# A third weight buffer from the first query on, four row buffers instead of five until the values, two engines' unit loops written out

## What is computed

```
q   = xn @ w_query                       # 8 heads, 2 x 128 each
s   = q . sub_keys                       # top 16 of 128, twice, then top 16 of 256
idx = e1 * 128 + e2                      # 8 x 16 experts of 16384 for each token
act = gelu(xn . expert_u[idx])
out = sum(gate * act * expert_v[idx])
```

## Time and profile before

| | |
|---|---|
| median of 3 runs | 4069.86 us (4068.22 to 4072.91) |
| profiled execution, its own time | 4066.02 us |
| span in its profile | 4063.9 us |
| PE busy in matmuls | 3865.1 us, 95% of the span |
| POOL / DVE / ACT busy | 2352.7 / 2448.9 / 1338.7 us |
| moved by DMA | 958.97 MB, mean 236 GB/s |
| mean granted clock of PE | 0.983 |

### The profile page before, as it was taken

One profiled execution on the slowest core, in us unless ns is written; L12 is line 12 of the kernel. 1 busy time (PEld: TensorE's weight loads), 2 busy tenths in 40 slices (PEclk: granted clock), 3 DMA queues, 4 the chain that ended last, 5 costly groups with the idle time before them and its releaser, 6 DMA issues.

```text
span 4063.9 us, 67270 instructions
## 1 busy us (share of the span) xinstructions
PE 3865.1 (95%) x27521; PEld 3420.8 (84%) x27521; DVE 2448.9 (60%) x3532; ACT 1338.7 (33%) x1380; POOL 2352.7 (58%) x994
## 2 busy tenths in 40 slices
PE   7999999999999999989999989999988999999997
PEld 5777777777778777869999989899988999999997
DVE  4343344433473555146878789986446777776776
ACT  4332233322332222123333334443233333333333
POOL 5332233322333344436666676667778999998995
PEclk8999999999999999989999999999999999999999
DMA  3222222222222344235676789999989999998994
GB/s 116 103 77 82 89 87 84 82 89 82 83 98 99 110 147 161 97 122 217 257 277 259 276 334 421 421 359 369 371 327 406 405 398 407 399 406 326 415 406 175
DMA packets 216723, 958.97 MB, mean 236 GB/s; under 512 B 18328, under 2 KB 92312, under 8 KB 114352
## 3 DMA queue, kind: packets, MB, share of 16 engines
q1 hardware_dynamic: 126832, 478.30, 32.1%
q0 software_dynamic: 55296, 402.68, 24.0%
q10 hardware_dynamic: 34368, 74.69, 4.7%
HBM read 891.01 MB, written 64.52 MB: 235 GB/s over the span
## 4 chain that ended last, share of the span: by engine, by line
PE 64%; POOL 11%; DMA 10%; DVE 7%; issue 3%; ACT 2%; SPq 1%; ACTq 0%; POOLq 0%; DVEq 0%
PE ps L417 17%; PE ps L419 16%; PE ps L418 16%; POOL wl L408 6%; DMA rowb<-v_rows,idx 4%; DMA raw<-stream 3%; POOL wl L412 3%; PE ps L1706 2%; PE ps L2029 2%; DVE ps L1451 2%; PE ps L2031 1%; PE ps L2030 1%; DVE H L1448 1%; DMA stage<-v_rows,idx 1%; POOL rowb L686 1%
## 5 line engine op out<-in xcount | busy, mean ns | idle before, releaser
L412 POOL TENSOR_TENSOR wl<-raw,wh 128x2048 fp32r<-128x2048 f32 x268 | 1242.7, 4637 | 1441.8 <-ACT wh L393 1440.6
L417 PE MATMUL ps<-xh,wh 128*128 128x320 f32 (+1 forms) x3904 | 1420.8, 364 | 87.3 <-POOL wl L412 62.3
L419 PE MATMUL ps<-xh,wl 128*128 128x320 f32 (+1 forms) x3904 | 1375.0, 352 | 0.0
L418 PE MATMUL ps<-xl,wh 128*128 128x320 f32 (+1 forms) x3904 | 1374.6, 352 | 0.0
L417 PEld LDWEIGHTS ps<-xh,wh 128*128 128x128 f32 x3904 | 742.1, 190 | 192.4 <-issue 66.8
L393 ACT ACTIVATE wh<-raw 128x2048 fp32r<-128x2048 f32 x270 | 517.1, 1915 | 939.6 <-PE ps L419 737.9
L419 PEld LDWEIGHTS ps<-xh,wl 128*128 128x128 f32 x3904 | 741.5, 190 | 83.0
L418 PEld LDWEIGHTS ps<-xl,wh 128*128 128x128 f32 x3904 | 742.9, 190 | 81.2 <-issue 7.7
L2029 PE MATMUL ps<-gah,wh 128*128 128x320 f32 x2048 | 645.7, 315 | 55.3 <-POOL wl L408 23.7
L2031 PE MATMUL ps<-gah,wl 128*128 128x320 f32 x2048 | 634.7, 310 | 0.0
L2030 PE MATMUL ps<-gal,wh 128*128 128x320 f32 x2048 | 634.6, 310 | 0.0
(11 more groups left out here) (334 smaller groups left out, 3986.6 us busy)
## 6 DMA issues: line engine op xcount, KB each, us to landing
raw<-stream SPq DMA_DIRECT2D x396, 1024.0 KB
gelu_scratch<-preb ACTq DMA_DIRECT2D x128, 160.0 KB
gates_scratch<-stage ACTq DMA_DIRECT2D x10, 2048.0 KB
gt<-gates_scratch SPq DMA_DIRECT2D x32, 640.0 KB
act<-gelu_scratch SPq DMA_DIRECT2D x32, 640.0 KB
mergegate_scratch<-sgb ACTq DMA_DIRECT2D x32, 256.0 KB, 2.0
sgm<-mergegate_scratch SPq DMA_DIRECT2D x32, 256.0 KB, 2.7
h_in<-x_t SPq DMA_DIRECT2D x4, 1024.0 KB, 7.8
```

Of the source, the lines that this page charges most:

```text
L412: pool.tensor_tensor(wl[s][:, :], raw[s][:, :], wh[s][:, :].bitcast(F32), ALU.subtract).then_inc(w_lo, 1)
L417: pe.matmul(dst, w_h, h[:, kx, lo:], start=start, stop=False)
L418: pe.matmul(dst, w_h, l[:, kx, lo:], start=False, stop=False)
L419: return pe.matmul(dst, w_l, h[:, kx, lo:], start=False, stop=stop)
```

## The change

The third buffer takes the memory of `rowb1` and serves from unit 124 on; `rowb1` moves to memory that `stage[0]` and a part of `stage[1]` hold until the gates are stored, and serves from j = 69 on. Up to j = 68 four row buffers are left, the quarters of H, so that fetch(n) waits for use(n - 4). Since the buffer of a unit is now its number modulo three, SP's loads and ACT's head and gate loops are written out. PE's loops and the order of `USED` are as before.

```
-    homes = range(ROWS_LOW if J_BACK <= FETCHED_AT[n] < J_HIGH else ROWS)
+    homes = (0, 2, 3, 4) if FETCHED_AT[n] < J_BACK else (0, 1) if FETCHED_AT[n] < J_HIGH else range(ROWS)
...
-        rows_low = [stage[1][:, NKEYS - D // GT:, :].rearrange("p e t -> p (e t)"), sb("rowb1", [P, D])[:, :]]
+        row_0 = stage[1][:, NKEYS - D // GT:, :].rearrange("p e t -> p (e t)")
+        raw_late = raw + [sb("raw2", [P, 2048])]
...
-        raw_v = raw + [sb("raw2", [P, 2048])]
+        row_1 = sb("rowb1", [P, D])
...
+            return quarter_h(max(b - 1, 0)) if FETCHED_AT[n] < J_BACK else row_0 if b == 0 else row_1[:, :] if b == 1 else rows_high[b - ROWS_LOW][:, :]
...
+        def load_late(sp, n):
+            k = n - U_QUERY
+            sp.wait_ge(w_lo, n - 1 if k < 2 else U_QUERY if k == 2 else n - 2)
+            sp.dma_start(raw_late[k % 3][:, :], stream[n]).then_inc(w_loaded[k % 3], 16)
+
+        def late_hi(act, n):
+            k = n - U_QUERY
+            act.wait_ge(w_loaded[k % 3], 16 * (k // 3 + 1) + (8 * U_QUERY if k % 3 < 2 else 0))
+            act.wait_ge(w_used, n - 1)
+            act.activation(wh[n % 2][:, :], raw_late[k % 3][:, :], ACT.Copy).then_inc(w_hi, 1)
+
+        def late_lo(pool, n):
+            pool.wait_ge(w_hi, n + 1)
+            pool.tensor_tensor(wl[n % 2][:, :], raw_late[(n - U_QUERY) % 3][:, :], wh[n % 2][:, :].bitcast(F32), ALU.subtract).then_inc(w_lo, 1)
...
-            with sp.Fori(0, (U_PEER - U_QUERY) // 2 - 4) as h:
-                for c in range(2):
-                    load_unit(sp, U_QUERY + 2 * h + c, c)
+            for n in range(U_QUERY, U_PEER - LOADS_LAST):
+                load_late(sp, n)
...
             load_group(0, 0)
-            for n in range(U_PEER - 8, U_PEER):
-                load_unit(sp, n, n % 2)
+            for n in range(U_PEER - LOADS_LAST, U_PEER):
+                load_late(sp, n)
...
             for j in range(F_ALL):
-                split_lo(pool, score_unit(SC_GATES) + j, j % 2)
+                late_lo(pool, score_unit(SC_GATES) + j)
...
                     if j >= J_BACK:
-                        pool.wait_ge(gates_stored[1], 16 + 8 * GB)
+                        for s in range(2):
+                            pool.wait_ge(gates_stored[s], 16 + 8 * GB)
...
-            with act.Fori(1, HEADS) as h:
+            for h in range(1, HEADS):
                 act_route(h)
...
-            with act.Fori(0, GATES_TWO // per) as b:
+            for b in range(GATES_TWO // per):
...
-            with act.Fori(GATES_TWO // per, GB // 2) as b:
+            for b in range(GATES_TWO // per, GB // 2):
```

More of the change, by code:

```diff
@@ L122 @@
 LAST_IN_H = max(n for n in range(2 * ALL) if FETCHED_AT[n] < J_BACK)
-R_GATED = F_REST - 5
+R_GATED, LOADS_LAST = F_REST - 5, 8
 def score_unit(e):
@@ L326, in row_buffer @@
             b = ROW_AT[n]
-            return rows_low[b] if b == 1 else quarter_h(max(b - 1, 0)) if FETCHED_AT[n] < J_BACK else rows_low[0] if b == 0 else rows_high[b - ROWS_LOW][:, :]
+            return quarter_h(max(b - 1, 0)) if FETCHED_AT[n] < J_BACK else row_0 if b == 0 else row_1[:, :] if b == 1 else rows_high[b - ROWS_LOW][:, :]
         gt, act_, gah, gal = (gt_0, gt_1), (act_0, act_1), (gah_0, gah_1), (gal_0, gal_1)
@@ L588, in _ @@
             load_group(0, 0)
-            for n in range(U_PEER - 8, U_PEER):
-                load_unit(sp, n, n % 2)
+            for n in range(U_PEER - LOADS_LAST, U_PEER):
+                load_late(sp, n)
             def load_values(g, s, ahead=True, first=False):
                 for c in range(NC4):
-                    load_value(sp, NC4 * g + c)
+                    load_late(sp, U_PEER + NC4 * g + c)
                     if c == 3 and ahead:
@@ L690, in _ @@
                 for c in range(PER_HEAD):
-                    split_lo(pool, U_QUERY + PER_HEAD * h + c, c % 2)
+                    late_lo(pool, U_QUERY + PER_HEAD * h + c)
                     for i in EARLY_AT.get(c, ()) if h else ():
@@ L698, in _ @@
             for m, n in enumerate(range(U_ROUTED, score_unit(SC_GATES))):
-                split_lo(pool, n, n % 2)
+                late_lo(pool, n)
                 for i in EARLY_AT.get(m, ()):
@@ L729, in _ @@
                 g, c = divmod(k, NC4)
-                value_lo(pool, k)
+                late_lo(pool, U_PEER + k)
                 if k == 1:
@@ L1018, in _, with act_ahead @@
                 act.dma_start(h_d[c], quarter_h(c)).then_inc(h_moved[c], 16)
-            def act_ahead(e, s, n, w=None):
+            def act_ahead(e, s, n):
                 act.wait_ge(w_used, n + 1)
-                split_hi(act, n + 2, s if w is None else w)
+                late_hi(act, n + 2)
                 act.wait_ge(pre_stored[s], 8 * e + 16 - 8 * s)
@@ L1033, in act_route @@
                 n = U_QUERY + PER_HEAD * h
-                score = lambda i: act_ahead(SC_HEAD * h + i, i % 2, n + SCORE_PLACE[i], SCORE_PLACE[i] % 2)
+                score = lambda i: act_ahead(SC_HEAD * h + i, i % 2, n + SCORE_PLACE[i])
                 for c in range(2):
                     act.wait_ge(w_used, n + 2 * c + 1)
-                    split_hi(act, n + 2 * c + 2, 0)
+                    late_hi(act, n + 2 * c + 2)
                     if not first:
@@ L1124, in act_values @@
                         act_halves(g + 1, 1 - s, e)
-                    value_hi(act, NC4 * g + c + 2)
+                    late_hi(act, U_PEER + NC4 * g + c + 2)
                     if then and c == 2:
```

## The result

The changed kernel takes 4135.4 us (median of 4 runs, 4132.57 to 4136.48) where the kernel before takes 4071.4 beside it: a ratio of 1.0159, 95% interval 1.0144 to 1.0173. It is slower by 64 us; in the two profiled executions the span grew by 70.1 us, from 4063.9 to 4134.0. The two differ mainly because the profiled execution of the kernel before (4066.0) is some 5 us faster than its median. Forecast was 4138.

A forecast was written before the change was run, and what follows sets the result against it. It took PE to bound the heads, PE, DVE and DMA together the gate stage, late loads the later stretch. Terms 50 + 36 + 2 - 22 + 3 + 1 = +70 on 4066.0 us gave 4136, by the median 4138; range 4088 to 4172.

The forecast's parts named there:

- The row buffers: Gate stage, j = 0 to 25: with four buffers PE idles 4.17 us in each of 19 units, +50 us.
- ring: Gate stage, 19 units: a closed chain through PE, DVE and POOL, 13.01 us where a unit without a gap takes 8.84.
- the +12 kept for late landings: Gate stage, j = 0 to 25: allowance for rows landing late, 11.5 us, making the upper bound +62.
- The clock: Gate stage: PE at half clock behind each of 19 gaps, 1.9 us each, +36 us (0 to 45).
- Ahead of the gate stage: Before the first one-hot products: fetch 61 waits one use longer for a row, +2 us (0 to 4).
- The third weight buffer: From 2720 to 3053 us: earlier loads remove PE's gaps until DMA is full, -22 us (-33 to -8).
- the smaller terms of +3 and +1: +3 us for four buffers at j = 28 to 66; +1 us for row 194's longer wait, from j = 69 on.
- Four buffers from j = 28 on: j = 28 to 66: a buffer less takes about one use off the room, +3 us (0 to +10).
- Written-out loops: SP's loads and ACT's head and gate loops: 0 us, bounds -3 and +8.
- The clock doesn't fall: Rival, gate stage: the chain holds but the clock stays up, +34 us, 4102 us; chance 0.17.
- The third buffer gives nothing: Rival, later stretch: beside a full DMA PE's 28 us of gaps stay, +92 us, 4160 us; chance 0.12.
- The rows' wait doesn't bind: Rival, gate stage: POOL's waits only mirror full DMA engines, the kernel gets faster, 4048 us; chance 0.08.

The follow-up runs named there:

- e6: e5 with 18 matmuls more, their result unused, behind each of 19 gate-stage units to fill PE's gaps: 1.0099 of the kernel before, 4105.3 us.
- e1: The kernel before with four row buffers up to j = 68 and nothing else of the change: 1.0231 of the kernel before.
- e2: The changed kernel with DVE using a unit's first row ahead of its first one-hots, the second between the two sets: 0.9967 of the kernel before.
- e5: The changed kernel with PE's loop over the gate stage's units 2 to 27 written out: 1.0172 of the kernel before, 4136.8 us.
- e4: The kernel before with SP's loads and ACT's head and gate loops written out: 0.999 of the kernel before.
- e7: The changed kernel with five row and two weight buffers up to j = 27, then four and three: 0.9949 of the kernel before, 4045.5 us.

## Why the prediction was right, point by point

- **The row buffers.** The prediction's list of 19 units and its ring held exactly: 19 gaps, at the units named. A ring of 13.01 us was put together from rows of before; e6 shows 13.08. Its term of +50 measured 54, from e6's 329.4 us against 275.4 (28 units, where the prediction spoke of 26), or up to 58 against the other kernels with five buffers. In the changed gate stage no wait of DVE for a row's landing is listed, so nothing of the +12 kept for late landings came. The prediction read POOL's wait for rows before as 53.5 us; it was 68.7, as shown above, and no term rested on it. e1 shows that nothing else of the change is in it, e2 that it is the place of the use in DVE's order and not the number of buffers alone.
- **The clock.** +36 was forecast and 31 measured (e5 against e6), by a price of 1.9 us for each gap; it measured 1.6. The gaps were 3.4 to 3.9 us in 18 of 19, not 4.17, because the half clock stretches PE's unit as well as DVE's start: in the turn shown PE works 10.45 us where a unit takes 8.84, while the whole turn grows only from 13.08 to 14.31. (The 19th gap, 5.0 us, comes again in e1, e5 and e6, 1.2 to 1.5 us longer than the others; why is open.) All 19 together made 0.89 of a granted clock, inside the 0.8 to 0.9 named. That a gap of this length brings the lower of the two levels had stood on two single gaps; it held in a steady row of them: the 4 us behind each of the 19 have a granted clock of 0.50 to 0.68.
- **Ahead of the gate stage.** +2 was forecast, +5.4 measured. Some 1.3 us of it aren't the change's: PE's first matmul on a weight unit that the change touches starts that much later already (1785.13 against 1783.79). The step that was short: fetch 57 waits one use longer too, not fetch 61 alone. PE's gap behind 57 grew from 3.88 (behind ACT) to 6.04 us (behind POOL's split), the one behind 61 hardly (2.96 to 3.06). Behind the second gap PE takes some 3 us longer to the first one-hot products without a longer wait: it is busy for 27.05 us (2377 to 2407.6) where it was for 23.95 (2375 to 2402), at a granted clock of 0.89 against 1.00. So a good half of the +5.4 is the clock's; what lowered it there wasn't tried by itself.
- **The third weight buffer.** -22 was forecast and, for it and the smaller terms of +3 and +1 together, -18.5 measured (-20.5 and +2.0, where the three had made -18); e1 against the changed kernel gives -21.1 for the third buffer alone, and the means over the ten traces -17.5. DMA at 0.96 is what is next. The edit only lets a load start earlier, and with that ACT's waits for loads fell from 80.7 to 12.5 us: the start had been too late, and the DMA engines, busy 0.93 of the time, had room for the earlier one. The Trainium skill's rule that transfers of all queues share the same 16 engines ("Trainium Kernel Development and Optimization", Key Constraints) had been set against this term. No trace here contradicts the rule, but a term near 0 doesn't follow from it where the engines aren't quite full.
- **Four buffers from j = 28 on.** +3 was taken, and e1 shows 375.7 us for 375.1: nothing that can be told, since the same part differs by more among the kernels with two weight buffers (369.1 to 375.7).
- **Written-out loops.** 0 was forecast; e4 shows 0.999 with 1 inside its interval. That ACT loses 4.43 us at each loop edge was a wrong reading, without weight in the sum.
- **The rivals.** *The clock doesn't fall* fell with e6. *The third buffer gives nothing* fell with e1, e2 and e7. *The rows' wait doesn't bind* fell with the result; its own condition, a use early enough in the unit, is what e2 brought about, and there the kernel is faster (a median of 4055.8; the rival had 4048).

Of the signs named, one was missed: PE's gaps in the later stretch came down to 11.8 us and not under 10. The others came: the 26 units took some 341 us (358.6 less two of 8.84), POOL waited 146.2 for DVE's rows, the clock was 0.89, ACT's waits for loads 12.5, and the 333 us of the later stretch became some 312 (less the 20.5).

The sum by parts, 5.4 + 83.2 - 20.5 + 2.0 = 70.1, against a forecast of 70 is luck to some us. The clock was set 5 us too high, the ring 4 and the first part 3 too low. The 70.1 also rest on one pair of executions: between the medians the change is 64 us, where the forecast of 4138 had meant 68 over the median of then.

## What to carry to other kernels

A buffer's worth is read from the instruction that frees it: list for each request what it waits for, and where that stands in the other engine's order. One buffer less can close a ring through three engines (here PE, DVE, POOL) though none of them is full, and moving the freeing instruction ahead of its engine's wait for PE opened the ring again at no cost in memory. When a change makes short, regular gaps on TensorE, price the half clock behind them too: here it was more than a third of the gate stage's loss.

## What the runs showed of the hardware that wasn't expected

Gaps of some 1.4 us in 19 of 28 units left the granted clock at 0.99 (e6), gaps of 3.5 to 4 us (one of 5.5) brought it to 0.89 (e5), and adding 342 matmuls made the kernel 31 us faster. Idle time that the profile puts down to "issue" at a loop's edge can be a wait that would be there anyway: with the loop written out it stayed at 4.6 us and changed only its name (e4).
